# Order of the first rows and weights, idle products ahead of them, and the squares of the gating stage in one transformer kernel

## The chip, the cores and the metric

One core of a Trainium2 chip runs the whole kernel in one launch. The metric is the device time in microseconds (us) of that launch. TensorE (PE in the profile) multiplies, ScalarE (ACT) evaluates functions and copies, VectorE (DVE) does elementwise work, GpSimd (POOL) does a little elementwise work, and the queue of SyncE (SP) issues nearly all transfers from the chip's memory.

## The reference

Two blocks follow each other on one sequence of 512 positions and 2048 features, all in float32. Every row norm is an rms norm over the features.

```python
h = rmsnorm(x, norm_mix_g);  u = h @ w_in                 # 2048 -> 12288, ten parts
ya = b_g * causal_dwconv3(c_g * xa, conv_w) * silu(za)
log_f, kk = gates of fl;  o = hgrn2_chunked(silu(q), kk, iv, log_f)   # 8 heads
yb = head_norm(o) * hg_norm_g * silu(og)
m = sigmoid(ga) * (ya @ w_a_out) + sigmoid(gb) * (yb @ w_b_out)
x = x + m @ w_o
gate = sigmoid(rmsnorm(x, ple_norm_g) @ w_ple_gate)       # the gating stage
x = x + gate * (p @ w_ple_proj)
x = rmsnorm(x, final_norm_g)
# second block
h = rms_norm(x, g) * (1 + scale) + shift                  # scale, shift, gate from silu(c) @ w_ada
proj = h @ w_in_2                                         # attention (8 heads), retention (4 heads)
x = rms_norm(x + gate * (y @ w_out_2), final_gain_2)
```

## The kernel before, in words

Data lie transposed: a "row" k is 128 features on the partitions by 512 positions. Each float32 operand is split in two, a high part cast to the reduced type fp32r (XH for data, WH for weights) and the remainder (XL, WL). A product is three TensorE products: high with high, low data with high weights, high data with low weights.

The work is a list of groups (`_plan`, L153). A group multiplies 16 rows (8 or 2 for some) with 512 weight columns and fills four banks of the product memory, so a group of 16 rows is 16 x 4 x 3 = 192 products. A unit is two rows of weights, so a group has eight units and three unit buffers stand in WH and WL, four in RAW. `pe_dense` (L295) writes the products of a group in steps k = 0 to 15: in an even step k, rows k and k+1 into banks 0 and 1, in an odd step the same two rows into banks 2 and 3. With `fed=True` the rows are still being made while the group runs, so steps 0 and 1 take one row each into all four banks. For each row and bank the loop at L319 issues the three products one after the other. Ahead of the first it waits for both halves of the row (`xhi`, `xlo`), ahead of the third for WL.

`act_dense` (L338) casts WH on ScalarE (L354), `dve_dense` (L359) subtracts to get WL on VectorE (L375), and `sp_dense` loads RAW. Each goes through the same steps k. In a step it first makes the weight units that `hi_upto` (L201) or `lo_upto` (L205) asks for, then the rows of data that its feed asks for, and then one piece of each of two queues of side work (`Turns`, L113): `chores`, a piece every step, and `specials`, at the rate `pace`. Every engine executes its instructions in the written order, so what stands ahead in a step delays what stands behind it.

At the start (group ("fl", 0)) the rows are x itself times a gain: ScalarE casts XH (L454) and squares the row (L459), VectorE makes XL (L475) and adds up the squares (L483). `start_part` (L513) is the special that asks for rows faster than the group does, up to 16 rows by its seventh piece. It then runs the bounds of the gates (`bound_act`, `bound_dve`, nine tiny VectorE operations), and the first row norm: one product with ones (L399, `norm0_pe`), its `rsqrt_dve` (L410) and `rsqrt_act` (L403), and then the normed rows of the next group ("q", 0) (L500, L490, L504). TensorE issues nothing until the first rows and weights are there.

The gating stage is the groups ("gate", 0) to ("gate", 3), on eight units each. After each of them ScalarE evaluates four sigmoids (L1630), VectorE multiplies and adds into x (L1922, L1926), and ScalarE writes for each of the four new rows two squares (L1650), plain and times a gain. POOL adds each up (L2019) and the square buffers are single, so a square waits until POOL has added the one before. For the last group ScalarE makes four squares only (L1637), and TensorE takes them as they are. After group 2 VectorE makes nine small weight tiles WG (L1929 to L1935). Behind the last group TensorE sums the squares (L1453 to L1463, twelve records of 512 columns until the first sum is complete), `rsqrt_dve` and `rsqrt_act` with the key r_12 turn the sum into a factor, VectorE makes three tiny vectors GG, GF (L1939 to L1943), and then the rows of the second block follow (L1095, L1080, L1100) for ("qr", 0), which is a group with `fed=True`. `rsqrt_act` first waits for its input and then asks for its function table.

Of the kernel before, what the change touches and what calls it, by code (L numbers as in the profile page):

```python
# [199 lines left out]

def hi_upto(n, k):  # L201
    return min(n + AHEAD if n or k else 0, len(UNITS) - 1) + 1


def lo_upto(n, k):  # L205
    return min(hi_upto(n, k), n + AHEAD + k % 2 if n else 3)

# [9 lines left out]
def build(nc, xT, pT, vec, logits, cst, masks, ident, w_in, w_a, w_b, w_o, w_gate, w_proj,  # L217
# [77 lines left out]
    def pe_dense(name, xh, xl, ready, swap=False, kmap=None, fed=False, cols=slice(0, 512)):  # L295
# [6 lines left out]
        for k in range(nk):  # L302
            n = FIRST[name] + k // 2
            s = n % NSPL
            if fed and k < 2:
                work = [(k, i) for i in range(4)]
            else:
                work = [(k - k % 2 + j, i + k % 2 * 2) for i in range(2) for j in range(2)]
            for q, i in work:
# [9 lines left out]
                for j, (l, r) in enumerate(pairs):  # L319
                    if j == 0:  # L320
                        T.wait_ge(hi, (yield hi, n if n or q else "first"))
                        T.wait_ge(xhi, (yield xhi, (ready, kk)))
                        T.wait_ge(xlo, (yield xlo, (ready, kk)))
                        if q == 0 and gone[i]:
                            T.wait_ge(gone[i][0], (yield gone[i]))
                    if j == 2:
                        T.wait_ge(lo, (yield lo, n if n or q else "first"))
                    first, final = q == 0 and j == 0, q == nk - 1 and j == 2
                    ins = nc.tensor.matmul(bank[b][:, cols], l, r[:, cols], start=first, stop=final)  # L329
                    done = [(name, i)] * (j == 2 and q == nk - 1)  # L330
                    done += [("unit", n)] * (j == 2 and k % 2 == 1 and (q, i) == work[-1])
                    if done:
                        ins.then_inc(dense.sem, dense.step(*done))
# [68 lines left out]

    def rsqrt_act(key, m, y):  # L403
        A.wait_ge(dve, (yield dve, (key, "m")))
        A.use(LNEXP)
        nc.scalar.activation(y, m, ACT.Ln).then_inc(act.sem, act.step((key, "ln")))
# [20 lines left out]
    SC = sb("SC", [5, 512], F32, 73728 + 11 * 2048)  # L427
    xv = xT.rearrange("(k p) s -> p k s", p=128)
    XLOADS = ([0], [1], [2, 3], [4, 5, 6], [7, 8, 9, 10], [11, 12, 13, 14, 15])
    xload = {k: ld[f"x{ks[0]}"] for ks in XLOADS for k in ks}  # L430

# [18 lines left out]
    def feed_raw_act():  # L450
        A.wait_ge(ld["vec"], (yield ld["vec"], 0))
        for k in range(16):
            A.wait_ge(xload[k], (yield xload[k], 0))
            nc.scalar.activation(XH1[:, k], X0[:, k], ACT.Copy, scale=vcol("mix_g", k)  # L454
                                 ).then_inc(xhi.sem, xhi.step(("raw", k)))
            for j in range(k - 1 if k else 16, 16 if k == 15 else k):
                if j > 2:
                    A.wait_ge(dve, (yield dve, ("acc0", j - 2)))
                nc.scalar.activation(SC[:, j % 2 if j else 2], X0[:, j], ACT.Square  # L459
                                     ).then_inc(act.sem, act.step(("sq0", j)))  # L460
# [10 lines left out]
    def feed_raw_dve():  # L471
        V.wait_ge(ld["vec"], (yield ld["vec"], 0))
        for k in range(16):
# [4 lines left out]
            for j in range(k - 2, 16 if k == 15 else k - 1):  # L478
                if j > 0:
                    V.wait_ge(act, (yield act, ("sq0", j)))  # L480
                    if j > 1:
                        V.wait_ge(dve, (yield dve, ("acc0", j - 1)))
                    nc.vector.tensor_tensor(SC[:, 2], SC[:, 2], SC[:, j % 2], ALU.add  # L483
                                            ).then_inc(dve.sem, dve.step(("acc0", j)))
# [28 lines left out]
    def start_part(eng, bound, norm):  # L513
        for n in range(7):
            if eng in raw_feed:
                yield from raw_feed[eng].upto(min(16, 2 * n + 4))
            yield
        if bound:
            yield from bound
        yield  # L520
        yield
        if eng == "pe":
            yield
        yield from norm
        yield
        for n in range(1, 7):
            if eng in h_feed:
                yield from h_feed[eng].upto(n)
            yield
# [872 lines left out]
    def pe():  # L1402
        shared[0] = True
        turns = pe_turns
        turns.specials.append(start_part("pe", None, norm0_pe()))
        yield from pe_dense(("fl", 0), XH1, XL1, "raw", fed=True)
# [101 lines left out]
    def act_program():  # L1508
# [112 lines left out]
        for g in range(4):  # L1621
            yield from act_dense(("gate", g), g_feed["act"])
            for i in range(4):
# [3 lines left out]
                else:  # L1627
                    A.wait_ge(xlo, (yield xlo, ("g", 12 + i)))
                A.use(SIG)
                nc.scalar.activation(GT[:, i], bank[banks["gate", g][i]][:, :], ACT.Sigmoid  # L1630
                                     ).then_inc(ev_a.sem, ev_a.step((("gate", g), i)))
            for i in range(4):
                j = 4 * g + i
                A.wait_ge(dve, (yield dve, ("x2", j)))
                if g == 3:
                    A.wait_ge(dense, (yield dense, (("proj", 3), 3)))
                    nc.scalar.activation(SQ2[:, 2 + i], X1[:, j], ACT.Square  # L1637
                                         ).then_inc(act.sem, act.step(("sq2", j)))
                    continue
                for u in range(2):  # L1640
                    scale = vcol("fin_g", j) if u else 1.0
                    if j == 0:
                        A.wait_ge(side, (yield side, ("r_ple", "sum")))
                        dst = AC[:, u]
                    else:
                        A.wait_ge(dense, (yield dense, (("proj", 3), 3)))
                        if j > 1:
                            A.wait_ge(pool, (yield pool, ("acc2u", u, j - 1)))
                        dst = SQ2[:, u]
                    nc.scalar.activation(dst, X1[:, j], ACT.Square, scale=scale  # L1650
                                         ).then_inc(act.sem, act.step(("sq2u", u, j)))
        yield from rsqrt_act("r_12", NN[:, 0], R12)
# [87 lines left out]
        for h in range(2):  # L1740
# [10 lines left out]
            else:  # L1751
                yield from to_end(out_norm_act(1))

    def out_norm_act(h):
        if h == 0:
# [55 lines left out]
    def first_norm_dve():  # L1811
        yield from idle(4)
        V.wait_ge(dve, (yield dve, ("r_12", "r")))
        yield from rsqrt_dve("r_1", 1.0 / D, NN[:, 0], R1, NN[:, 2])

    def dve_program():
# [94 lines left out]
        for g in range(4):  # L1911
            yield from dve_dense(("proj", g))
            if g == 0:
                yield from rsqrt_dve("r_ple", 1.0 / D, NN[:, 0], NN[:, 1], NN[:, 2])
                turns.specials.append(rows_of(g_feed["dve"], 16))
        for g in range(4):
            yield from dve_dense(("gate", g), g_feed["dve"])
            for i in range(4):
# [8 lines left out]
                                        ).then_inc(dve.sem, dve.step(("x2", j)))  # L1927
            if g == 2:
                nc.vector.tensor_scalar(WG[:, 4], ONES[:, :], EPS, None, ALU.mult  # L1929
                                        ).then_inc(dve.sem, dve.step())  # L1930
                for i in range(4):
                    nc.vector.tensor_scalar(WG[:, i], ONES[:, :], vcol("fin_g", 12 + i), vcol("fin_g", 12 + i),
                                            ALU.mult, ALU.mult).then_inc(dve.sem, dve.step(("wg", i)))
                    V.wait_ge(dve, (yield dve, ("wg", i)))
                    nc.vector.tensor_scalar(WG[:, i], WG[:, i], EPS, None, ALU.add  # L1935
                                            ).then_inc(dve.sem, dve.step(*(["wg"] if i == 3 else [])))
        yield from rsqrt_dve("r_12", 1.0 / D, NN[:, 0], R12, NN[:, 2], eps=EPS * EPS)
        V.wait_ge(dve, (yield dve, "mod"))
        nc.vector.tensor_scalar(GG, MOD[:, 16:32], 1.0, None, ALU.add).then_inc(dve.sem, dve.step("gg0"))  # L1939
        V.wait_ge(dve, (yield dve, "gg0"))  # L1940
        nc.vector.tensor_tensor(GG, GG, vall("ng"), ALU.mult).then_inc(dve.sem, dve.step("gg"))
        V.wait_ge(dve, (yield dve, "gg"))
        nc.vector.tensor_tensor(GF, GG, vall("fin_g"), ALU.mult).then_inc(dve.sem, dve.step("gf"))  # L1943
        turns.specials.append(first_norm_dve())
# [220 lines left out]
```

## Time and profile before

| | us |
|---|---|
| median of 3 runs (lowest, highest) | 2627.98 (2627.77, 2628.41) |
| the profiled execution | 2625.84 |
| its span, from first to last instruction | 2624.5 |
| PE busy in the span | 2593.7 (99%) |
| DVE busy | 1265.5 (48%) |
| ACT busy | 892.0 (34%) |
| POOL busy | 73.7 (3%) |
| transfers | 309.18 MB, 118 GB/s on average |

Times of the rows below come from the one profiled execution. They start at the span's beginning. "PEld" is the load of the stationary operand on TensorE, which runs beside the products. A duration of TensorE is that of one pipelined product; products issued back to back start at a closer distance than their duration.

### The profile page before, as it was taken

How to read it: one execution, taken by the hardware profiler on the slowest of the kernel's cores; microseconds unless marked ns; L12 is line 12 of the kernel's file. 1: busy time of each engine (PE TensorE's matmuls, PEld its weight loads, DVE VectorE, ACT ScalarE, POOL GpSimd, SP SyncE). 2: the span in 40 equal slices, each digit the busy share in tenths (PEclk: the TensorE clock that was granted, in tenths of full speed). 3: DMA queues.
4: the chain of work that ended last, by engine and by line, in shares of the span. 5: the costliest groups of instructions: out<-in, count | busy, mean ns of one | idle time of the engine just before them, and what ended most of it. 6: DMA issues, size and time to landing. Idle time of an engine off the chain costs nothing.

```text
span 2624.5 us, 29678 instructions
## 1 busy us (share of the span) xinstructions
PE 2593.7 (99%) x12166; PEld 2095.4 (80%) x12166; DVE 1265.5 (48%) x2013; ACT 892.0 (34%) x1236; POOL 73.7 (3%) x64
## 2 busy tenths in 40 slices
PE   8999999999999999999999999999999999999998
PEld 7888888878888888888888888688777777777888
DVE  7556634468334555655443453552243434443425
ACT  5643324333222222222322443332232343433323
POOL 0000000000000000000001111100000000000000
PEclk9999999999999999999999999999999999999999
DMA  5322233222334666666442222234222222222424
GB/s 194 101 76 78 81 97 97 89 73 81 89 96 147 217 216 207 216 213 213 136 161 97 94 99 97 73 125 145 85 72 64 89 72 81 73 73 84 165 97 153
DMA packets 159976, 309.18 MB, mean 118 GB/s; under 512 B 11040, under 2 KB 15392, under 8 KB 158816
## 3 DMA queue, kind: packets, MB, share of 16 engines
q1 hardware_dynamic: 159040, 305.70, 36.1%
q8 instruction: 96, 1.57, 0.2%
q0 software_dynamic: 224, 1.15, 0.1%
q10 hardware_dynamic: 576, 0.43, 0.1%
q14 instruction: 40, 0.33, 0.0%
HBM read 298.84 MB, written 8.39 MB: 117 GB/s over the span
## 4 chain that ended last, share of the span: by engine, by line
PE 94%; DVE 2%; issue 2%; ACT 1%; DMA 0%; POOL 0%; SPq 0%; DVEq 0%; ACTq 0%; POOLq 0%
PE bank L329 87%; PE bank L1276 1%; PE bank L1167 1%; PE bank L1250 1%; PE bank L702 1%; PE bank L754 1%; PE bank L1265 1%; PE bank L1156 1%; PE bank L399 0%; DVE WL L375 0%; ACT WH L354 0%; DVE SC L483 0%; DMA X<-in_xT 0%; DVE Y L1980 0%; PE bank L692 0%
## 5 line engine op out<-in xcount | busy, mean ns | idle before, releaser
L329 PE MATMUL bank<-XH,WH 128*128 128x512 f32 (+1 forms) x2880 | 1145.6, 398 | 12.2 <-DVE XL L475 5.5
L329 PE MATMUL bank<-XH,WL 128*128 128x512 f32 (+1 forms) x2880 | 1111.7, 386 | 5.5 <-DVE WL L375 5.5
L329 PE MATMUL bank<-XL,WH 128*128 128x512 f32 (+1 forms) x2880 | 1109.9, 385 | 0.0
L375 DVE TENSOR_TENSOR WL<-RAW,WH 128x1024 fp32r<-128x1024 f32 x443 | 544.0, 1230 | 958.1 <-ACT WH L354 957.2
L354 ACT CAST WH<-RAW 128x1024 fp32r<-128x1024 f32 x443 | 463.9, 1049 | 1162.2 <-PE bank L329 1162.0
L329 PEld LDWEIGHTS bank<-XH,WH 128*128 128x128 f32 x2880 | 542.4, 188 | 135.1 <-issue 20.7
L329 PEld LDWEIGHTS bank<-XL,WH 128*128 128x128 f32 x2880 | 542.7, 188 | 119.3 <-issue 15.0
L329 PEld LDWEIGHTS bank<-XH,WL 128*128 128x128 f32 x2880 | 542.1, 188 | 116.9 <-DVE WL L375 7.2
L329 PE MATMUL bank<-WH,XH 128*128 128x512 f32 x384 | 155.6, 405 | 0.0
L329 PE MATMUL bank<-WL,XH 128*128 128x512 f32 x384 | 149.8, 390 | 0.0
L329 PE MATMUL bank<-WH,XL 128*128 128x512 f32 x384 | 149.5, 389 | 0.0
L1016 DVE CUSTOM_DVE_ANT_0 AST<-AST,CB 128x512 f32<-128x512 f32 x192 | 125.3, 687 | 10.8 <-DMA AST<-in_w_ada 10.8
L329 PE MATMUL bank<-YH,WH 128*128 128x512 f32 x256 | 101.0, 394 | 0.0
L329 PE MATMUL bank<-YH,WL 128*128 128x512 f32 x256 | 100.4, 392 | 0.0
L329 PE MATMUL bank<-YL,WH 128*128 128x512 f32 x256 | 99.5, 389 | 0.0
L329 PEld LDWEIGHTS bank<-WH,XL 128*128 128x128 f32 x384 | 72.2, 188 | 17.5 <-issue 3.1
L329 PEld LDWEIGHTS bank<-WH,XH 128*128 128x128 f32 x384 | 72.1, 188 | 17.4 <-issue 3.1
L329 PEld LDWEIGHTS bank<-WL,XH 128*128 128x128 f32 x384 | 72.1, 188 | 15.3
L1354 DVE CUSTOM_DVE_ANT_0 PP<-PP,CM 128x512 f32<-128x512 f32 x32 | 22.2, 692 | 79.9 <-ACT PP L1288 79.9
L1305 ACT COPY PT<-bank 128x512 f32<-128x512 f32 x32 | 18.7, 585 | 116.1 <-PE bank L1265 116.1
L329 PEld LDWEIGHTS bank<-YH,WL 128*128 128x128 f32 x256 | 48.1, 188 | 11.3
L329 PEld LDWEIGHTS bank<-YL,WH 128*128 128x128 f32 x256 | 48.1, 188 | 10.7
(252 smaller groups left out, 1634.5 us busy)
## 6 DMA issues: line engine op xcount, KB each, us to landing
RAW<-in_w_in SPq DMA_DIRECT2D x303, 512.0 KB, 3.6
AST<-in_w_ada SPq DMA_DIRECT2D x192, 256.0 KB, 4.1
RAW<-in_w_out SPq DMA_DIRECT2D x40, 512.0 KB, 3.5
RAW<-in_w_o SPq DMA_DIRECT2D x32, 512.0 KB, 3.5
RAW<-in_w_gate SPq DMA_DIRECT2D x32, 512.0 KB, 3.5
RAW<-in_w_a SPq DMA_DIRECT2D x16, 512.0 KB, 4.2
RAW<-in_w_b SPq DMA_DIRECT2D x16, 512.0 KB, 4.2
XT<-in_xT SPq DMA_DIRECT2D x4, 1024.0 KB, 7.4
```

What stands on the lines that cost most here:

```text
L329: ins = nc.tensor.matmul(bank[b][:, cols], l, r[:, cols], start=first, stop=final)
L354: nc.scalar.copy(WH[:, m % NSPL], RAW[:, m % NRAW]).then_inc(hi.sem, hi.step(m))
L375: nc.vector.tensor_tensor(WL[:, m % NSPL], RAW[:, m % NRAW], WH[:, m % NSPL].bitcast(F32), ALU.subtract).then_inc(lo.sem, lo.step(m))
L702: ins = nc.tensor.matmul(b[y:y + 64, 32 * n:32 * n + 32].rearrange("p (n x) -> p n x", x=h), t, late(t, lev), start=True, stop=True, tile_ ...
L754: ins = nc.tensor.matmul(b[:, 128 * c:512], VN[:, c, 128 * i:128 * i + 128], AT[:, 640 * c:512 * c + 512], start=c == 0, stop=c == 3)
L1016: nc.vector.tensor_tensor_reduce(AST[:, n % 3], AST[:, n % 3], CB[:, q % 2], 1.0, 0.0, ALU.mult, ALU.add, PART[:, n:n + 1]).then_inc(dve.s ...
L1156: nc.tensor.matmul(b[:, :], YY[:, 9 + 2 * r, 128 * c:128 * c + 128], YY[:, 8 + 2 * r], start=True, stop=True).then_inc(side.sem, side.step ...
L1167: ins = nc.tensor.matmul(b[:, :], V2[:, c, 256 * r + 128 * u:256 * r + 128 * u + 128], PT[:, c], start=c == 0, stop=c == 3)
L1250: nc.tensor.matmul(b[:, :], YY[:, h, 128 * i:128 * i + 128], K[:, j], start=True, stop=True).then_inc(side.sem, side.step(("as", h, i)))
L1265: ins = nc.tensor.transpose(b[:, 128 * c:128 * c + 128], PP[:, i % 2, 128 * c:128 * c + 128], IDN[:, :])
L1276: ins = nc.tensor.matmul(b[:, :], Vt[:, c, 128 * j:128 * j + 128], PT[:, c], start=c == 0, stop=c == 3)
L1354: nc.vector.tensor_tensor_reduce(P, P, CM[:, 2, 384 - 128 * i:896 - 128 * i], 1.0, 0.0, ALU.mult, ALU.add, st[:, 2:3]).then_inc(dve.sem, d ...
```

## The change

Six edits. Products of a fed group's first row are issued part by part over the four banks. The waits for XH and XL are separated. Rows and weight units of the first group are ordered anew on ScalarE and VectorE, the norm of the start comes ahead of the bounds, and a row's square is written later than the row, into four buffers. Eleven products of ones with ones, 128 columns each, stand ahead of the first group on TensorE, whose result is not read. In the gating stage the squares of groups 0 to 2 become a chore with one row in every second step of the next group, the weight tiles become a chore of group 1, and GG and GF move ahead of the stage. `rsqrt_act` asks for its table before it waits.

```diff
 def hi_upto(n, k):
+    if n < 2:
+        return k + 1
     return min(n + AHEAD if n or k else 0, len(UNITS) - 1) + 1
 def lo_upto(n, k):
-    return min(hi_upto(n, k), n + AHEAD + k % 2 if n else 3)
+    return hi_upto(n, k) if n < 2 else min(hi_upto(n, k), n + AHEAD + k % 2)
...
-            if fed and k < 2:
-                work = [(k, i) for i in range(4)]
+            if fed and k == 0:
+                work = [(0, i, (j,)) for j in range(3) for i in range(4)]
+            elif fed and k == 1:
+                work = [(1, i, (0, 1, 2)) for i in range(4)]
...
                     if j == 0:
                         T.wait_ge(hi, (yield hi, n if n or q else "first"))
                         T.wait_ge(xhi, (yield xhi, (ready, kk)))
-                        T.wait_ge(xlo, (yield xlo, (ready, kk)))
...
+                    if j == 1:
+                        T.wait_ge(xlo, (yield xlo, (ready, kk)))
...
     def rsqrt_act(key, m, y):
+        A.use(LNEXP)
         A.wait_ge(dve, (yield dve, (key, "m")))
-        A.use(LNEXP)
...
     # feed_raw_act, a row k of x
-            for j in range(k - 1 if k else 16, 16 if k == 15 else k):
-                if j > 2:
-                    A.wait_ge(dve, (yield dve, ("acc0", j - 2)))
-                nc.scalar.activation(SC[:, j % 2 if j else 2], X0[:, j], ACT.Square
+            for j in range(max(k - 2, 0) if k < 11 else k - 1, 16 if k == 15 else k if k > 9 else k - 1):
+                if j > 4:
+                    A.wait_ge(dve, (yield dve, ("acc0", j - 4)))
+                nc.scalar.activation(SC[:, SQ_AT[j % 4] if j else 2], X0[:, j], ACT.Square
...
     def start_part(eng, bound, norm):
-        for n in range(7):
+        for n in range(10):
             if eng in raw_feed:
-                yield from raw_feed[eng].upto(min(16, 2 * n + 4))
-            yield
-        if bound:
-            yield from bound
-        yield
-        yield
+                yield from raw_feed[eng].upto(2 * n + 2 if n < 4 else 4 + (4 * n + 1) // 3)
+            yield
         if eng == "pe":
             yield
         yield from norm
         yield
+        if bound:
+            yield from bound
         for n in range(1, 7):
...
     def pe():
+        T.wait_ge(dve, (yield dve, "ones"))
+        for n in range(11):
+            nc.tensor.matmul(bank[7][:, 0:128], ONES[:, :], ONES[:, :], start=True, stop=True)
...
-        yield from act_dense(("fl", 0), raw_feed["act"])
+        yield from act_dense(("fl", 0), raw_feed["act"], 1)
-        yield from dve_dense(("fl", 0), raw_feed["dve"])
+        yield from dve_dense(("fl", 0), raw_feed["dve"], 1)
...
     # act_program, after each of the groups ("gate", g)
-            for i in range(4):
-                ... (both squares of the row, each behind its waits)
+            if g < 3:
+                turns.chores.append(squares_act(g))
+                continue
+            yield from turns.finish(turns.chores)
+            ... (the four squares of g == 3)
+    def squares_act(g):
+        for j in range(4 * g, 4 * g + 4):
+            ... (the same two squares and waits)
+            yield
+            yield
...
     # dve_program
+    def last_weights_dve():
+        yield from idle(4)
+        ... (WG[4], then WG[i] in two operations, a yield after each i)
+        ... (wait for "mod", then GG, GG, GF, ahead of the loop over the gate groups)
         for g in range(4):
             yield from dve_dense(("gate", g), g_feed["dve"])
...
-            if g == 2:
-                ... (WG[4] and WG[i])
+            if g == 0:
+                turns.chores.append(last_weights_dve())
+        yield from turns.finish(turns.chores)
         yield from rsqrt_dve("r_12", 1.0 / D, NN[:, 0], R12, NN[:, 2], eps=EPS * EPS)
-        ... (wait for "mod", GG, GG, GF)
```

## Rows read from the trace of the kernel before

**Rows 1.** The page, part 1: busy time, share of span, instructions.
```profile
PE 2593.7 (99%) x12166; PEld 2095.4 (80%) x12166; DVE 1265.5 (48%) x2013; ACT 892.0 (34%) x1236; POOL 73.7 (3%) x64
```
**Rows 2.** Waits of PE, whole span: us in total, times, longest us.
```profile
PE bank L329 <- DVE XL L475: 5.5, 1, 5.5
PE bank L329 <- DVE WL L375: 5.5, 4, 2.3
PE bank L329 <- ACT WH L354: 0.5, 2, 0.3
```
**Rows 3.** Windows: stretch, busy us (x) by engine, granted clock, DMA share, GB/s.
```profile
35.10:37.90 2.80, 0.49 (x4) 0.06 (x2) 2.60 (x4) 0.63 (x1) 0.00 (x0) 1.00 0.01 3
1699.00:1702.50 3.50, 3.50 (x9) 2.76 (x10) 3.50 (x6) 1.45 (x2) 0.00 (x0) 0.51 0.00 0
```
**Rows 4.** Timeline of the start: start us, us, engine line op [idle before <-releaser].
```profile
0.84 0.17 DVE L1818 MEMSET ONES<- 128x128 f32 x1 [0.84 <-PEq L2158]
...
4.42 0.60 ACT L347 CAST WH<-RAW 128x512 fp32r<-128x512 f32 x1
...
5.53 0.77 PE L329 MATMUL bank<-XH,WH 128*128 128x512 f32 x1 [5.53 <-DVE XL L475]
...
9.50 0.40 PE L329 MATMUL bank<-XH,WH 128*128 128x512 f32 x1
```
**Rows 5.** Timeline, from the end of the first raw rows to the first norm.
```profile
36.59 1.22 DVE L375 TENSOR_TENSOR WL<-RAW,WH 128x1024 fp32r<-128x1024 f32 x1
37.73 0.16 DVE L550 TENSOR_TENSOR SM<-V 128x8 f32<-128x8 f32 x1
...
37.87 0.51 PE L329 MATMUL bank<-XH,WL 128*128 128x512 f32 x1 [2.31 <-DVE WL L375]
...
40.29 1.02 PE L399 MATMUL bank<-SC,ONES 128*128 128x512 f32 x2
...
41.63 0.68 DVE L412 TENSOR_SCALAR SC<-bank 128x512 f32<-128x512 f32 x1
...
45.86 1.29 DVE L500 TENSOR_TENSOR X<-X,R 128x512 f32<-128x512 f32 x2
```
**Rows 6.** Groups of DVE by line, 4 to 38 us: busy us, mean ns, idle before.
```profile
L475 DVE SCALAR_TENSOR_TENSOR XL<-X,V,XH 128x512 fp32r<-128x512 f32 x16 | 12.0, 749 | 8.6 <-ACT XH L454 8.6
L483 DVE TENSOR_TENSOR SC<-SC 128x512 f32<-128x512 f32 x15 | 10.3, 688 | 0.2
```
**Rows 7.** Timeline of PE: first products of ("q", 0) and of ("iv", 0).
```profile
54.89 0.40 PE L329 MATMUL bank<-XH,WH 128*128 128x512 f32 x1
...
98.46 0.39 PE L329 MATMUL bank<-WH,XH 128*128 128x512 f32 x1
```
**Rows 8.** Timeline of the gating stage, groups 2 and 3.
```profile
1606.60 0.50 PE L329 MATMUL bank<-XH,WL 128*128 128x512 f32 x1 [1.15 <-DVE WL L375]
...
1640.31 10.65 POOL L2019 TENSOR_TENSOR AC<-AC,SQ 128x512 f32<-128x512 f32 x8 [34.85 <-ACT SQ L1650]
...
1649.13 2.92 ACT L354 CAST WH<-RAW 128x1024 fp32r<-128x1024 f32 x3
...
1652.75 0.50 PE L329 MATMUL bank<-XH,WL 128*128 128x512 f32 x1 [1.80 <-DVE WL L375]
```
**Rows 9.** Timeline from the end of the gating stage into ("qr", 0).
```profile
1690.43 0.69 DVE L412 TENSOR_SCALAR NN<-bank 128x512 f32<-128x512 f32 x1 [2.91 <-PE bank L1457]
...
1691.15 1.28 ACT L64 ACT_TABLE_LOAD   x1 [2.96 <-DVE NN L412]
...
1695.83 0.17 DVE L1939 TENSOR_SCALAR SM<-MOD 128x16 f32<-128x16 f32 x1
...
1696.45 1.41 DVE L1095 SCALAR_TENSOR_TENSOR GT<-X,SM,NN 128x512 f32<-128x512 f32 x2
1697.24 1.38 ACT L1080 ACTIVATE XH<-GT,MOD 128x512 fp32r<-128x512 f32 x2 [2.57 <-DVE GT L1095]
...
1699.00 0.70 PE L329 MATMUL bank<-XH,WH 128*128 128x512 f32 x1 [4.31 <-DVE XL L1100]
```

More of the change, by code:

```diff
@@ L304, in pe_dense @@
             s = n % NSPL
-            if fed and k < 2:
-                work = [(k, i) for i in range(4)]
-            else:
-                work = [(k - k % 2 + j, i + k % 2 * 2) for i in range(2) for j in range(2)]
-            for q, i in work:
+            if fed and k == 0:
+                work = [(0, i, (j,)) for j in range(3) for i in range(4)]
+            elif fed and k == 1:
+                work = [(1, i, (0, 1, 2)) for i in range(4)]
+            else:
+                work = [(k - k % 2 + j, i + k % 2 * 2, (0, 1, 2)) for i in range(2) for j in range(2)]
+            for q, i, parts in work:
                 kk = kmap[q] if kmap else q
@@ L318, in pe_dense @@
                              (WL[:, s, q % 2, c], xh[:, kk])]
-                for j, (l, r) in enumerate(pairs):
+                for j in parts:
+                    l, r = pairs[j]
                     if j == 0:
@@ L330, in pe_dense @@
                     done = [(name, i)] * (j == 2 and q == nk - 1)
-                    done += [("unit", n)] * (j == 2 and k % 2 == 1 and (q, i) == work[-1])
+                    done += [("unit", n)] * (j == 2 and k % 2 == 1 and (q, i) == work[-1][:2])
                     if done:
@@ L428, in build @@
     xv = xT.rearrange("(k p) s -> p k s", p=128)
+    SQ_AT = (0, 1, 3, 4)
     XLOADS = ([0], [1], [2, 3], [4, 5, 6], [7, 8, 9, 10], [11, 12, 13, 14, 15])
@@ L482, in feed_raw_dve @@
                         V.wait_ge(dve, (yield dve, ("acc0", j - 1)))
-                    nc.vector.tensor_tensor(SC[:, 2], SC[:, 2], SC[:, j % 2], ALU.add
+                    nc.vector.tensor_tensor(SC[:, 2], SC[:, 2], SC[:, SQ_AT[j % 4]], ALU.add
                                             ).then_inc(dve.sem, dve.step(("acc0", j)))
@@ L1631, in act_program @@
                                      ).then_inc(ev_a.sem, ev_a.step((("gate", g), i)))
-            for i in range(4):
[L1633 to L1651, printed above, removed]
+            if g < 3:
+                turns.chores.append(squares_act(g))
+                continue
+            yield from turns.finish(turns.chores)
+            A.wait_ge(dense, (yield dense, (("proj", 3), 3)))
+            for i in range(4):
+                A.wait_ge(dve, (yield dve, ("x2", 12 + i)))
+                nc.scalar.activation(SQ2[:, 2 + i], X1[:, 12 + i], ACT.Square
+                                     ).then_inc(act.sem, act.step(("sq2", 12 + i)))
         yield from rsqrt_act("r_12", NN[:, 0], R12)
@@ L1752, in act_program @@
                 yield from to_end(out_norm_act(1))
+    def squares_act(g):
+        for j in range(4 * g, 4 * g + 4):
+            A.wait_ge(dve, (yield dve, ("x2", j)))
+            for u in range(2):
+                scale = vcol("fin_g", j) if u else 1.0
+                if j == 0:
+                    A.wait_ge(side, (yield side, ("r_ple", "sum")))
+                    dst = AC[:, u]
+                else:
+                    A.wait_ge(dense, (yield dense, (("proj", 3), 3)))
+                    if j > 1:
+                        A.wait_ge(pool, (yield pool, ("acc2u", u, j - 1)))
+                    dst = SQ2[:, u]
+                nc.scalar.activation(dst, X1[:, j], ACT.Square, scale=scale
+                                     ).then_inc(act.sem, act.step(("sq2u", u, j)))
+            yield
+            yield
     def out_norm_act(h):
@@ L1814, in first_norm_dve @@
         yield from rsqrt_dve("r_1", 1.0 / D, NN[:, 0], R1, NN[:, 2])
+    def last_weights_dve():
+        yield from idle(4)
+        nc.vector.tensor_scalar(WG[:, 4], ONES[:, :], EPS, None, ALU.mult
+                                ).then_inc(dve.sem, dve.step())
+        for i in range(4):
+            nc.vector.tensor_scalar(WG[:, i], ONES[:, :], vcol("fin_g", 12 + i), vcol("fin_g", 12 + i),
+                                    ALU.mult, ALU.mult).then_inc(dve.sem, dve.step(("wg", i)))
+            V.wait_ge(dve, (yield dve, ("wg", i)))
+            nc.vector.tensor_scalar(WG[:, i], WG[:, i], EPS, None, ALU.add
+                                    ).then_inc(dve.sem, dve.step(*(["wg"] if i == 3 else [])))
+            yield
     def dve_program():
@@ L1915, in dve_program @@
                 turns.specials.append(rows_of(g_feed["dve"], 16))
+        V.wait_ge(dve, (yield dve, "mod"))
+        nc.vector.tensor_scalar(GG, MOD[:, 16:32], 1.0, None, ALU.add).then_inc(dve.sem, dve.step("gg0"))
+        V.wait_ge(dve, (yield dve, "gg0"))
+        nc.vector.tensor_tensor(GG, GG, vall("ng"), ALU.mult).then_inc(dve.sem, dve.step("gg"))
+        V.wait_ge(dve, (yield dve, "gg"))
+        nc.vector.tensor_tensor(GF, GG, vall("fin_g"), ALU.mult).then_inc(dve.sem, dve.step("gf"))
         for g in range(4):
@@ L1927, in dve_program @@
                                         ).then_inc(dve.sem, dve.step(("x2", j)))
-            if g == 2:
-                nc.vector.tensor_scalar(WG[:, 4], ONES[:, :], EPS, None, ALU.mult
-                                        ).then_inc(dve.sem, dve.step())
-                for i in range(4):
[L1932 to L1936, printed above, removed]
-        yield from rsqrt_dve("r_12", 1.0 / D, NN[:, 0], R12, NN[:, 2], eps=EPS * EPS)
[L1938 to L1943, printed above, removed]
+            if g == 0:
+                turns.chores.append(last_weights_dve())
+        yield from turns.finish(turns.chores)
+        yield from rsqrt_dve("r_12", 1.0 / D, NN[:, 0], R12, NN[:, 2], eps=EPS * EPS)
         turns.specials.append(first_norm_dve())
```

## The prediction

> **What bounds the kernel now.** I read the page's busy shares first: TensorE is busy for 2593.7 of 2624.5 us [rows 1], so only its idle stretches and stretches at half clock can be won, some 31 us plus those. Then TensorE's waits over the whole span [rows 2], which name the stretches that the change touches: 5.5 us for XL at the start, four waits for WL with 5.5 us (the longest, 2.3, in the first group), two for WH with 0.5 us, and then the timeline at each place, and the granted clock beside it.
>
> The regular distance comes from ("q", 0), which runs without a break: (98.46 - 54.89)/192 = 0.227 us [rows 7]. An idle bracket counts from the modelled end of the last product (0.39 to 0.40 us after its start), so a wait costs its bracket plus 0.16 us, plus about 0.1 us for a slower first distance behind it, say 0.27 in all.
>
> **The start, products and clock.** The first product stands at 5.53 us, released by XL, though WH was cast at 4.42 + 0.60 = 5.02 [rows 4]. Nine products take until 9.50: 3.97 us in place of 9 x 0.227 = 2.04. That is the distance of 1.2 GHz, so 1.93 us are lost. The change removes the wait for XL from the first four products and puts eleven idle ones ahead, which can begin at about 1.1 us, when ONES is written [rows 4]. Their price: a pair of records of 512 columns takes 1.02 us with a duration of 0.59 each, so a start distance of 0.43 and 0.86 for one whole product at 2.4 GHz [rows 5]; 128 columns are a quarter of it, 0.21 us, or 0.43 at 1.2 GHz (estimates from that row). If the clock rises as long after the first activity as it did before, 3.97 us, it rises at 5.1, with 9.3 of the eleven done; the rest ends at about 5.5. The first real product starts there, at full clock. Gain 1.9 us. Bounds: the clock doesn't rise from such short products, and the eleven take 4.7 us and push the start to 5.8: 0.3 us lost; or it rises at once at the earliest the data allow, 2.3 us gained. I take 1.9, the value with the rise at the distance that the row has.
> The Trainium skill (TensorE: Matmul & The Clock Gate, Part 1) says that warming up is counted in time and not in matmuls, and that its moment varies from run to run; by that rule the rise comes after the eleven have ended in some runs, and each product until then takes twice its time. The trace has one start only and can't show that spread.
>
> **The start, order of rows.** In the first group TensorE stops once: 2.31 us until 37.87, for the WL of 36.59 [rows 5], 2.58 us in all by the rule above. That WL is unit 5, and it stood behind all sixteen rows, because `start_part` asks for 16 rows by its seventh piece. A row costs VectorE 0.75 us for XL and 0.69 for the sum [rows 6], about 1.26 when packed. With the new order unit 5 stands behind row 11 in place of row 15. Following the queues step by step with the same durations: unit 4's WH still waits for its transfer, which is queued behind all of x, and then WH is cast before rows 8 to 10. WL of units 4, 5 and 6 end near 25, 30 and 35 us, where TensorE wants them at 28, 33 and 39. So this stop goes: 2.6 us.
> What is late next is the norm. It stands on TensorE behind step 11, about 38.4 us; the last sum of squares ends near 37.9, so it doesn't wait. From its issue to the normed rows VectorE and ScalarE took 41.63 to 45.86, 4.2 us [rows 5], begun 0.6 us later than need be because a WL stood ahead. Now WL of unit 7 stands behind that chain. It ends near 38.4 + 1.1 + 4.2 + 1.15 = 44.9, and TensorE wants it about 6.5 us after the norm's issue, at 45.0. Behind it come the bounds (before: nine tiny operations from 37.73 [rows 5], about 2.2 us with ScalarE's answers), now in front of the normed rows and of units 8 to 10. These end at about 51.9, 55.6 and 61.7, wanted at 51.9, 55.7 and 61.3. Three margins of nearly nothing: I take 0.4 us lost. Bounds: nothing, or one stop as long as the old one, 2.6.
> ("q", 0) then starts near 50.8 in place of 54.89: the start is worth 1.9 + 2.6 - 0.4 = 4.1 us. After that ScalarE's casts are released unit by unit by TensorE, so all of the rest moves with it.
>
> **The gating stage.** ScalarE casts three WH in a row at 1649.13 because eight squares stood ahead of them, in lockstep with POOL's single buffer (eight additions, 10.65 us [rows 8]). TensorE then waits at unit 2 of the next group, once for WH and once for WL. Groups 2 and 3: brackets 1.15 and 1.80 for WL [rows 8], for WH two waits with 0.5 together [rows 2]. Group 1: what rows 2 leave for the fourth WL wait, 5.5 - 2.31 - 1.15 - 1.80 = 0.2. With 0.27 for each of the five waits: 3.65 + 1.35 = 5.0 us. As chores, a row's two squares come behind the casts, every second step of 2.7 us. POOL needs 10.65/4 = 2.7 us for a row's two additions and has 5.4. VectorE's weight tiles go to steps 4 to 7 of group 1, where it has nothing but one WL per two steps. ScalarE's next WH is cast right after the sigmoids, four steps before it is wanted. POOL's additions now lie beside WL subtractions; the one slowed WL costs nothing as it is wanted two steps later. Without that cover it would be one addition, 1.3 us, a unit. I take 5.0 gained; bounds 5.0 and 2.0 (one wait per boundary of 0.7 stays).
>
> **The border to the second block.** The sum is complete for VectorE at 1690.43. Then the function table, 1.28 us at 1691.15, stands in the chain [rows 9]; ScalarE is done with its squares 2 us earlier, so the load moves beside TensorE's products: 1.28. GG and GF stand between 1695.83 and 1696.45: 0.62. XH of the first row is then ready 1.90 us earlier, at 1697.24 + 0.71 - 1.90 = 1696.05, and the first product needs only that. It starts at about 1696.25 in place of 1699.00: 2.75 us. XL of row 0 follows 0.8 us behind XH, and four products take 0.9: at full clock just in time; row 3 is wanted at 1702.6 and ready at 1701.9. Bounds: 1.9 (if the start still hangs on XL) and 2.75; I take 2.75.
> The clock: in 1699.00 to 1702.50 the granted clock is 0.51 [rows 3], so 1.2 GHz, after TensorE had done nothing for 4.31 us [rows 9]. The other idle stretch, 2.31 us [rows 5], left it at 1.00 [rows 3]. The new one is about 1.6 us, on the side of the second. Eight intervals took 3.48 in place of 1.82 us: 1.6 gained; bounds 0 and 1.6.
> The same page of the Trainium skill (HAM oscillation) warns of idle gaps in TensorE's work as what brings the low clock back; the two stretches above agree with a limit that lies between them.
>
> Border: 2.75 + 1.6 = 4.35 us.
>
> **Sum.** 4.1 + 5.0 + 4.35 = 13.45 us. The profiled execution took 2625.84, its span 2624.5; both would be 13.4 less, 2612.4 and 2611.1. The runs' median is 2627.98, 2.1 above the profiled one, in which I see nothing that the change touches: 2627.98 - 13.45 = 2614.5.
> Other fed groups ("wb", "wo", "out") only get their first row's waits later, and their banks up to 1.4 us sooner, which the bank turnover has room for: nothing.
>
> **Rivals.**
> (a) *The clock doesn't follow.* One or both half-clock stretches stay: 1.6 at the border gives 2616.1, 1.9 to 2.2 at the start 2616.4 to 2616.7, both up to 2618.3. For: there is one row only of a rise and one of a fall, and idle products of 128 columns are not in the trace. Against: TensorE is as busy with them as with others. The moment that the rule above leaves open belongs here too.
> (b) *VectorE becomes the bound at the start.* The norm's chain and the bounds now stand ahead of units 7 to 10; if each comes late, TensorE stops again and gets back what it gained, 2.6 us or, with the bounds' 2.2 on the way, the whole 4.1: 2617.1 to 2618.6. For: margins under 0.5 us. Against: TensorE itself releases that chain, so it doesn't grow.
> (c) *The waits were hidden anyway*, or the chores move them to the last group, where ScalarE must finish them before the final squares: no change beyond the start's half, 2623 to 2628. Against: the chores are through by step 8 of sixteen.
> (d) *Slower.* The casts fall into lockstep with TensorE: with less lead in units 0 to 3 each unit is cast, subtracted and used in turn, and WH plus WL, 1.0 + 1.2 us, stand open for every unit. It takes over the sign from 13.45/2.2 = 6 units on; over the sixteen of ("fl", 0) and ("q", 0) it costs 35 us, so 2650. Against: from unit 4 on `hi_upto` is as it was, and ScalarE and VectorE sat idle 8.6 us for each other in the first 38 us [rows 6].
>
> **How the numbers follow.** Forecast 0.62, with its own range 2612.5 to 2616; (a) 0.18; (b) 0.13; (c) 0.04; (d) 0.03. The range holds the forecast, (a) and most of (b): 2611.5 to 2618. A change under 0.2% (5.3 us) can't be told from none. The forecast, (a) and (b) are all beyond it: faster 0.93, same 0.04, slower 0.03.
>
> **What would show it.** Right: first dense product near 5.5 with distances of 0.23 at once; no stop before the norm; ("q", 0) starting near 50.8; no waits for WH or WL in the gating stage; no table load between the first sum and its logarithm; TensorE idle for 1.5 to 2 us at the border, at a granted clock of 1.00. Wrong: distances of 0.43 after 5.5 or at the border (a); waits for WL between 44 and 62 us (b); waits at the gating stage's group starts (c).

## The result, and the profile after

The changed kernel takes 2612.01 us (median of 4 runs, 2611.78 to 2612.64), the kernel before 2628.19 beside it (4 runs, 2627.77 to 2630.15). The ratio is 0.9937, 95% interval 0.9920 to 0.9955: 16.2 us less. The profiled execution of the changed kernel is its slowest, 2612.64, with a span of 2611.3; that of the kernel before was faster than its runs. Between the two spans lie only 13.2 us. "Idle" below is the time in brackets in a row of a profile: from the modelled end of TensorE's last product to the next start.

Waits of TensorE, whole span (us in total, times, longest), for [rows 2]:
```profile
PE bank L1270 <- ACT PP L1302: 2.1, 2, 1.0
PE bank L335 <- issue: 1.6, 1, 1.6
PE bank L335 <- DVE Y L2001: 1.5, 2, 1.2
PE bank L1412 <- DVE ONES L1845: 1.1, 1, 1.1
```
Ahead of the attention one wait for a row is left, the 1.6 us at the border (listed as "issue"), and a short one behind it, at the ninth row of ("qr", 0). The timeline of the start, for [rows 4, 5, 7]:
```profile
1.06 5.06 PE L1412 MATMUL bank<-ONES 128*128 128x128 f32 x22 [1.06 <-DVE ONES L1845]
...
4.48 0.60 ACT L353 CAST WH<-RAW 128x512 fp32r<-128x512 f32 x1
...
5.77 1.74 PE L335 MATMUL bank<-XH,WH 128*128 128x512 f32 x4
...
7.35 1.09 PE L335 MATMUL bank<-XL,WH 128*128 128x512 f32 x4
...
39.41 1.02 PE L405 MATMUL bank<-SC,ONES 128*128 128x512 f32 x2
...
40.46 0.69 DVE L418 TENSOR_SCALAR SC<-bank 128x512 f32<-128x512 f32 x1 [1.66 <-PE bank L405]
...
47.82 1.29 DVE L507 TENSOR_TENSOR X<-X,R 128x512 f32<-128x512 f32 x2
...
51.26 1.10 PE L335 MATMUL bank<-XH,WH 128*128 128x512 f32 x4
...
51.53 1.22 DVE L381 TENSOR_TENSOR WL<-RAW,WH 128x1024 fp32r<-128x1024 f32 x1
...
53.12 0.62 PE L335 MATMUL bank<-XH,WL 128*128 128x512 f32 x2
```
The idle products run at 0.43 us each (two records of 0.21), and the first four dense ones take 1.58 us until the next four start, in place of 0.91: the granted clock rose at 7.02, 6.0 us after TensorE's first activity at 1.06. In the profile before it rose at 9.48, 4.0 us after the first product. ("q", 0) starts at 51.26, 3.63 earlier. WL of unit 8 ends at 52.75, 0.4 us before it is wanted.

The gating stage's group 3, for [rows 8]. The cast follows the last sigmoid, the squares come behind it:
```profile
1633.06 0.60 ACT L1638 ACTIVATE GT<-bank 128x512 f32<-128x512 f32 x1 [0.76 <-PE bank L335]
...
1633.55 1.05 ACT L360 CAST WH<-RAW 128x1024 fp32r<-128x1024 f32 x1
...
1634.49 0.63 ACT L1764 ACTIVATE SQ<-X 128x512 f32<-128x512 f32 x1
...
1635.20 2.37 POOL L2040 TENSOR_TENSOR AC<-AC,SQ 128x512 f32<-128x512 f32 x1 [24.60 <-ACT SQ L1764]
1635.21 1.22 DVE L381 TENSOR_TENSOR WL<-RAW,WH 128x1024 fp32r<-128x1024 f32 x1
```
The border, for [rows 9]. The table is loaded beside the products, and the first product follows XH:
```profile
1679.49 1.28 ACT L64 ACT_TABLE_LOAD   x1
...
1681.72 0.69 DVE L418 TENSOR_SCALAR NN<-bank 128x512 f32<-128x512 f32 x1 [2.92 <-PE bank L1465]
...
1682.45 0.63 ACT L412 ACTIVATE NN<-NN 128x512 f32<-128x512 f32 x1 [1.68 <-DVE NN L418]
...
1686.74 1.39 ACT L1085 ACTIVATE XH<-GT,MOD 128x512 fp32r<-128x512 f32 x2 [2.06 <-DVE GT L1100]
...
1687.56 1.17 PE L335 MATMUL bank<-XH,WH 128*128 128x512 f32 x4 [1.58 <-issue]
```
And the granted clock around it (stretch, busy by engine in the order PE, PEld, DVE, ACT, POOL, then clock, DMA share, GB/s), for [rows 3]:
```profile
1685.50:1687.60 2.10, 0.52 (x3) 0.07 (x1) 1.94 (x4) 0.86 (x2) 0.00 (x0) 1.00 0.00 0
1687.60:1692.00 4.40, 4.40 (x20) 3.61 (x21) 4.40 (x7) 1.97 (x3) 0.00 (x0) 1.00 0.00 0
```
Where the 13.3 us between the two profiles arise, by the start of the same dense product in both: 3.6 up to ("iv", 0), nothing more until the second gating group ("gate", 1), then 0.5, 2.0 and 2.65 at its three boundaries, 4.3 at the border (2.74 of idle time, 1.56 of half clock) and 0.25 at the ninth row behind it, and nothing from there to the end.

### The profile page after: what moved, and what is told of

Read it like the earlier page. It is cut to its first block, busy times and chain, and to the rows that moved or that the text cites. A ratio compares the mean times of both kernels' runs of the same rounds, so it can differ in the third digit from the quotient of the medians.

```text
span 2611.3 us, 29657 instructions
## 1 busy us (share of the span) xinstructions
PE 2594.0 (99%) x12188; PEld 2097.4 (80%) x12188; DVE 1259.8 (48%) x2013; ACT 889.7 (34%) x1236; POOL 79.0 (3%) x64
## 3 DMA queue, kind: packets, MB, share of 16 engines
q0 software_dynamic: 224, 1.15, 0.1%
## 4 chain that ended last, share of the span: by engine, by line
PE 99%; DVE 1%; ACT 0%; issue 0%
PE bank L335 91%; PE bank L1281 1%; PE bank L1172 1%; PE bank L1255 1%; PE bank L707 1%; PE bank L759 1%; PE bank L405 1%; PE bank L1270 1%; PE bank L1161 1%; PE bank L1412 0%; DVE Y L2001 0%; PE bank L697 0%; PE bank L715 0%; DVE X L1800 0%; PE bank L729 0%; PE bank L1512 0%
```

## The experiments

Twelve kernels. Median (lowest to highest) of n runs, and the median of the kernel before on the same chip:

| kernel | us | n | before | ratio, 95% |
|---|---|---|---|---|
| b_again | 2627.79 (2625.75 to 2630.21) | 11 | 2627.70 | 1.0001, 0.9992 to 1.0010 |
| b_idle | 2628.18 (2626.11 to 2630.12) | 11 | 2627.70 | 1.0000, 0.9992 to 1.0009 |
| b_order | 2626.34 (2624.05 to 2627.23) | 11 | 2627.70 | 0.9997, 0.9988 to 1.0006 |
| b_start | 2620.92 (2618.97 to 2624.17) | 11 | 2628.41 | 0.9973, 0.9964 to 0.9982 |
| b_gate | 2623.45 (2620.61 to 2624.49) | 11 | 2627.98 | 0.9980, 0.9971 to 0.9989 |
| b_border | 2625.25 (2624.55 to 2628.60) | 11 | 2627.98 | 0.9989, 0.9981 to 0.9998 |
| a_noidle | 2613.32 (2613.06 to 2613.44) | 5 | 2627.70 | 0.9945, 0.9932 to 0.9959 |
| a_oldorder | 2617.36 (2616.51 to 2617.63) | 5 | 2628.41 | 0.9957, 0.9945 to 0.9970 |
| a_fedold | 2615.09 (2614.66 to 2616.59) | 5 | 2627.98 | 0.9951, 0.9937 to 0.9964 |
| a_gateold | 2617.58 (2616.80 to 2619.22) | 5 | 2628.41 | 0.9960, 0.9947 to 0.9972 |
| a_tablelate | 2615.23 (2613.04 to 2615.40) | 5 | 2627.98 | 0.9947, 0.9935 to 0.9960 |
| a_best | 2611.70 (2611.42 to 2612.38) | 5 | 2628.41 | 0.9937, 0.9924 to 0.9949 |

The interval of a ratio is about 2.5 us wide to each side, with five runs 3.4. So b_idle and b_order can't be told from none by their times; there the profiles decide. What the kernels named a_ lose is said against the changed kernel's 2612.01, which ran on another chip; the median of the kernel before differs by up to 0.7 us between the chips.

**b_again**: before, unchanged.

> The kernel before, once more, for a second and third start of it. Theory S (the moment at which the clock rises varies from run to run, and the profiled execution of before had an early one, 3.97 us after the first product): this profile shows more than nine products at the distance of 0.43 us, up to sixteen, and the times scatter by 1 to 2 us between 2626 and 2628.5. Rival U (the 2.1 us between the profiled execution and the median of before come from something else, the same in each run): nine products at 0.43 again, and all times near 2628.

The clock rose at 10.31, 4.7 us after the first product at 5.59, against 4.0 in the profile before; at half clock the 0.8 us later cost 0.4. But the times scatter over 4.5 us. S is right in kind and its place is wrong: over all fourteen profiles the rise came 2.9 to 6.0 us after TensorE's first activity, which is worth about 1.5 us at half clock. U falls too.

**b_idle**: before with the idle products.
```diff
+        T.wait_ge(dve, (yield dve, "ones"))
+        for n in range(11):
+            nc.tensor.matmul(bank[7][:, 0:128], ONES[:, :], ONES[:, :], start=True, stop=True)
```

> The kernel before with the eleven idle products alone. By the two profiles the first dense product then stands at 5.8 us, 0.25 later, and three dense products are slow in place of nine: 1.0 us faster, 2627 beside 2628.2. Theory S: the median gains more than the profile shows, 1.5 to 2.5 us, because late rises of the clock are what the products take away. Rival U: 1.0 us. Rival V (the idle products give nothing, the row's order does it all): 0 or 0.3 us slower.

V comes nearest, for a reason that it didn't name. The products work: the clock rose at 4.16, the first dense product starts at 5.66 at full clock, and the tenth is 1.6 us ahead of the profile before. TensorE then runs into rows and units that aren't made yet, and is slowed at 39 us; at ("iv", 0) it is 2.0 us behind. Timeline of PE, then windows as above:
```profile
12.61 0.50 PE L329 MATMUL bank<-XH,WH 128*128 128x512 f32 x1 [0.87 <-ACT WH L354]
...
13.87 0.51 PE L329 MATMUL bank<-XH,WL 128*128 128x512 f32 x1 [0.52 <-DVE WL L375]
...
38.44 0.79 PE L329 MATMUL bank<-XH,WL 128*128 128x512 f32 x1 [2.30 <-DVE WL L375]
```
```profile
38.50:41.90 3.40, 3.40 (x9) 2.68 (x10) 2.14 (x9) 1.44 (x4) 0.00 (x0) 0.53 0.54 154
...
1656.00:1659.50 3.50, 3.50 (x10) 2.68 (x10) 1.02 (x1) 0.00 (x0) 0.00 (x0) 0.53 0.78 258
...
1702.60:1707.40 4.80, 4.77 (x11) 3.80 (x12) 4.80 (x7) 1.44 (x2) 0.00 (x0) 0.50 0.04 8
```
Behind the same 2.3 us of idle time the clock had stayed at 1.00 in the profile before [rows 3]; the second window stands behind the 1.8 us in gating group 3, where that profile was at full clock too. This is what formed theory F. The third window is the border: the half clock lasts until 1707.4 there, 4.8 us of work, where the profile before had 3.4. b_gate shows the same.

**b_order**: before with `hi_upto`, `lo_upto`, the row feeds, the four square buffers and `start_part` of the change.

> The kernel before with the new order of rows, squares and weight units in the first group alone (hi_upto, lo_upto, the row feeds, the four square buffers, the norm ahead of the bounds). Theory: the stop of 2.3 us at 35 us goes and nothing comes in its place, 2.6 us faster, (q, 0) starts at 52.3 in place of 54.9. Rival (b) of the prediction: a stop comes back at units 7 to 10, 44 to 62 us, and less than 1 us is left.

Half right: the stop at 35 us is gone, but one comes back as the rival says, at WL of unit 8:
```profile
54.59 0.50 PE L331 MATMUL bank<-XH,WL 128*128 128x512 f32 x1 [0.93 <-DVE WL L377]
```
It is the third product of ("q", 0). In the changed kernel the part order asks for WL with the ninth, 1.4 us later. The clock also rose 1.7 us later here than in the profile before (11.14 against 9.48), and fell at 1653 us, behind the 1.8 us of gating group 3.

**a_noidle**: after without the idle products.

> The changed kernel without the idle products. Theory by the profiles: the first dense product then stands at about 5.15 us, since it needs only XH and WH, and some 9 of the products are slow, so 0.6 to 1.2 us slower than the changed kernel, 2613. Theory S: 1.5 to 2.5 us slower in the median. Rival V: nothing, or 0.6 us faster as the start comes earlier.

1.3 us slower in the medians, 0.75 in the profiles, with 0.4 us of scatter: the first dense product stands at 5.25, and the clock rose at 9.30. As the profiles said, and the times don't need S. But the two profiles drew unlike rises, 4.0 us after the first activity here and 6.0 in the changed kernel, so 0.75 us isn't what the products are worth in every execution.

**b_gate**: before with the squares and weight tiles as chores.

> The kernel before with the gating stage's squares and weight tiles as chores, nothing else. Theory: the five waits go, 5.1 us in the profile (the part of the stage in the profile of the changed kernel). Theory F, from the second batch of profiles (a stop of TensorE of about 2 us is followed by 3.4 us at half clock in some executions and not in others; each costs 1.6 us): two stops fewer, so the median gains more than 5.1, some 6 us, 2621.7, and the times scatter less than the 4 us of the kernel before. Rival: the clock doesn't depend on these stops, then exactly 5.1 and the same scatter.

4.5 us in the medians, 5.4 between the fastest runs on that chip. The five waits are gone, and over the gating stage the same products gain 5.1 us on the profile before: the theory's size. Its extra in the median didn't come (the interval, 2.9 to 7.6 us, leaves it open), and the scatter stayed at 3.9 us: in the profiled execution the clock fell behind the stop at 36 us and at the border all the same. This profile also bears out b_idle without idle products: its clock rose early, at 8.83, and TensorE ran into two waits, of 0.40 and 0.53 us at 13 and 14 us, which the profile before doesn't have.

**b_border**: before with the table load first, and GG and GF ahead of the stage.
```diff
     def rsqrt_act(key, m, y):
+        A.use(LNEXP)
         A.wait_ge(dve, (yield dve, (key, "m")))
-        A.use(LNEXP)
```

> The kernel before with the table load ahead of the wait and with GG and GF ahead of the stage, nothing else. Theory: 1.28 + 0.62 = 1.9 us less idle time at the border, 2.8 us in place of 4.7. Whether the 3.4 us at half clock behind it go: by my prediction they go in each execution (3.5 us faster in all), by theory F only in some (between 1.9 and 3.5 in the median, scatter of 2 us or more).

2.7 us, within theory F's span, though the interval (0.5 to 5.0 us) holds the prediction's 3.5 too. The border's idle time is 1.8 us shorter, 2.5 in place of 4.3, and in the profiled execution the clock still fell behind it, and behind gating group 3 as well. So what the expectation drew from the prediction, that the half clock goes in each execution, doesn't hold.

**a_tablelate**: after with that diff taken back.

> The changed kernel with the table load behind the wait again. Theory: the border's idle time grows by 1.28 us to 3.2, so 2613.3 at least. Theory F: in part of the executions the clock falls behind it, which costs 1.6 more there: times in two heaps, 2613.3 and 2614.9. Rival (a limit between 2.3 and 4.3 us, the same in each execution): one heap, scatter of 0.5 us.

3.2 us slower, and in line with F's two heaps, from five runs: one at 2613.04 with a mean clock of 0.999, four from 2614.88 to 2615.40, three of them at 0.998. The profile of a run of the upper heap, with 2.9 us of idle time ahead of 1688.74:
```profile
1685.50:1689.50 4.00, 1.13 (x4) 0.67 (x4) 3.77 (x7) 1.75 (x3) 0.00 (x0) 1.00 0.00 0
1689.50:1692.90 3.40, 3.40 (x10) 2.62 (x9) 3.40 (x5) 1.44 (x2) 0.00 (x0) 0.51 0.00 0
```

**a_fedold**: after with the parts of the first row in the old order and both waits ahead of the first.
```diff
-                work = [(0, i, (j,)) for j in range(3) for i in range(4)]
+                work = [(0, i, (0, 1, 2)) for i in range(4)]
...
+                        T.wait_ge(xlo, (yield xlo, (ready, kk)))
```

> The changed kernel with the first row's products in the old order (high, XL and WL of a bank in turn, both halves of the row waited for ahead of the first). Theory: WL of unit 8 comes late at the first row of (q, 0), as it does in the kernel before with the new order alone (a stop of 1.09 us there), and the border loses the 0.75 us by which XH leads XL: 1.8 us slower, 2613.8. Rival: the part order is worth nothing beyond the border, 0.8 us.

3.1 us slower. The profile has the wait for WL of unit 8 again (0.92 us idle until 53.01, 1.1 lost), 2.52 us idle at the border in place of 1.58, and 0.25 more at the ninth row of ("qr", 0); 2.5 in all, with the span at 2613.8. No clock fell behind the 2.52 here, where b_border's did. Two of five runs lie 1.5 to 1.9 above the rest.

**b_start**: before with all edits of the start.

> The kernel before with all three edits of the start (idle products, new order of rows and units, products of the first row part by part), the gating stage and the tables as before. The part order also reaches the border, 0.75 us. Theory: the three need each other, since the idle products alone ran into two waits for rows (1.0 and 0.7 us) and the order alone into one at unit 8 (1.1 us): by the two profiles 3.6 us at the start, 0.8 at the border and, with one stop fewer, less half clock, so 4.4 to 6 us in the median, 2622 to 2623.5, where the parts alone gave 0 and 1.4. Rival: the parts don't need each other, then about 2 us, 2626.

7.5 us (interval 4.7 to 9.5), more than expected. The profile gives 6.8: 4.1 at the start, the rest at the border. This fastest run has no fall at all, even behind 3.37 us of idle time at the border; 1.6 of its 6.8 us is the half clock that the profile before had there.

**a_oldorder**: after with the order of rows, squares and units taken back.

> The changed kernel with the old order of rows, squares and units in the first group. Theory: the stop of 2.5 us behind 35 us comes back, and with the idle products the rows and units are late at 11 to 14 us by some 1.5 us more; half clock behind one of them in part of the executions (1.6 us): 4 to 5.5 us slower, 2616 to 2617.5, with a scatter of 2 us. Rival: only the stop, 2.6 us, 2614.6.

5.4 us slower, the theory's upper end: waits of 1.52 and 0.52 us at 12 and 14, a third of 0.7 at 38, and half clock from 14.23 to 17.65. The profiled run is the fastest, 3.9 slower in span. Timeline of PE:
```profile
12.45 0.50 PE L333 MATMUL bank<-XH,WH 128*128 128x512 f32 x1 [1.52 <-ACT WH L358]
...
13.71 0.50 PE L333 MATMUL bank<-XH,WL 128*128 128x512 f32 x1 [0.52 <-DVE WL L379]
...
14.74 0.63 PE L333 MATMUL bank<-XH,WL 128*128 128x512 f32 x1
```

**a_gateold**: after with squares and weight tiles in their old place.

> The changed kernel with the squares and weight tiles of the gating stage in their old place. Theory: five waits of 5.1 us in all come back; two of them are stops of 1.3 and 2.0 us, and behind the longer one the clock falls in part of the executions: 5.1 to 6.7 us slower, 2617.1 to 2618.7, in two heaps. Rival: 5.1 us in each execution, scatter of 0.5 us.

5.6 us slower, from 4.8 to 7.2. Over the gating stage its profile loses 5.2 us, the theory's size, with no fall of the clock. The five runs show no clear heaps, and the highest lies above the theory's span.

**a_best**: after with two changes.
```diff
-        for n in range(11):
+        for n in range(9):
...
     # first_norm_act and first_norm_dve
-        yield from idle(4)
+        yield from idle(13)
```

> The changed kernel with nine idle products in place of eleven, and with the second norm of the border (r_1, 4.1 us of VectorE between the rows of (qr, 0)) moved from the fifth to the fourteenth piece of that group. Theory: the first dense product stands 0.5 us earlier, at half clock, which is worth 0.3 us; the wait of 0.5 us at the ninth row of (qr, 0) goes, as all sixteen rows are made by then: 0.8 us faster, 2611.2. Rival: with fewer idle products the clock rises later and takes it back, and the norm only moves the wait to the next group: 2612.

2611.70, 0.3 below the changed kernel's median, on another chip, so not told apart by the times. In the profile the wait at the ninth row is gone, worth 0.4 us. The first dense product stands at 5.51, and the clock had risen at 5.46, where the changed kernel's profile has 7.02: 0.8 us at the start, most of which may be the luck of one execution. The span is 2610.0.

## Why the prediction was right, step by step

The profile was met to 0.2 us (span 2611.3 for 2611.1). The median, 2612.01 for 2614.5, was missed by 2.5 us and lies below the forecast's own range, inside the whole range.

**The border** was right to a tenth in the two profiles: from VectorE's first operation on the sum to the first product it took 1699.00 - 1690.43 = 8.57 us and takes 5.84, so 2.73 for 2.75. With the clock at 1.00, 4.3 for 4.35.

**The gating stage**: 5.1 for 5.0. Shown from both sides by b_gate and a_gateold. The cover named for POOL's additions wasn't needed: the addition takes 2.37 us beside a WL subtraction, which keeps its 1.22. One part of the mechanism was left out. Behind group 2 WL waits not only for WH: VectorE's nine operations on the weight tiles end after the first WH is cast (1649.13 and about 1 us), while behind group 1 WL follows WH at once. Timeline of DVE before:
```profile
1604.69 4.11 DVE L375 TENSOR_TENSOR WL<-RAW,WH 128x1024 fp32r<-128x1024 f32 x3 [7.87 <-ACT WH L354]
...
1651.33 0.23 DVE L1935 TENSOR_SCALAR WG<-WG 128x128 f32<-128x128 f32 x1
1651.48 3.49 DVE L375 TENSOR_TENSOR WL<-RAW,WH 128x1024 fp32r<-128x1024 f32 x3
```
That boundary was worth 2.65 us and the one without tiles 2.0, so the tiles' own share is some 0.65 us (an estimate from the two). Squares and tiles were moved together in each run, so no run separates them.

**The start**: the stop at 35 us was 2.6 and is gone. The lateness of 0.4 didn't come, WL of unit 8 is on time by 0.4 us. The term that was mis-sized is the clock's, 1.9: nine dense products on, the gain is 1.0. The prediction let the clock rise as long after the first activity as before, and here it took 2 us longer. In the six other profiles with eleven idle products it rose 2.9 to 5.8 us after them, so 1.9 was one value of several. That the sum for the profile, 13.45, met 13.2 is in part luck: 0.9 too much for the clock stands against 0.4 for a lateness that didn't come, 0.25 at the ninth row, which the sum had left out, and 0.1 in the gating stage.

**The step that failed** is about the median: "2.1 above the profiled one, in which I see nothing that the change touches". The change touches it. The forecast took it that a stop of 2.31 us leaves the clock at 1.00 and that a limit lies between that and 4.31. The fourteen profiles, by the idle time of a stop:

| idle, us | profiles with that stop | half clock at it or behind it |
|---|---|---|
| 1.6 (border) | 5 | 0 |
| 1.8 (gating group 3) | 7 | 3 |
| 2.3 (start) | 5 | 2 |
| 2.5 (border) | 2 | 1 |
| 2.9 (border) | 1 | 1 |
| 3.4 (border) | 1 | 0 |
| 4.3 (border) | 5 | 5 |

a_oldorder adds a fall behind waits of 1.5 and 0.5 us close to each other. So no limit holds in each execution for stops of 1.8 to 3.4 us: the same stop is followed by half clock in some executions and not in others. A fall lasted 3.4 us and cost 1.6 to 1.7 us; at the border of b_idle and b_gate it lasted 6.8 us, 4.8 and 5.1 of them with TensorE at work. The profiled execution before had one fall, at the border.

The runs of the kernel before spread from 2625.8 to 2631.3, and the mean clock of a run goes with it. Of the 74 in the experiments 27 have 0.998 and 2626.6 us on average, 36 have 0.997 and 2628.4, and 11 have 0.996 and 2630.5: steps of about one fall. The changed kernel has one stop of 1.6 us left where the kernel before had four of 1.15 to 4.31 (besides three of 1.0 to 1.2 in the attention that both have), and all its four runs lie at 0.999 within 0.9 us. The medians are 3.0 us further apart than the spans. 2.35 of them is that the profiled execution before was faster than its median, about what one or two falls more would cost: these no longer come. The other 0.6 is that the changed kernel's profiled run was its slowest; its cause stays open. How often each stop is followed by a fall wasn't measured, and a run without a profile shows its falls only through its mean clock.

**Rivals.** (b) was the near one: alone (b_order) the order does turn into a stop at unit 8, and the part order, which the prediction priced at the border and at the first product only, is what holds it off. Taken out (a_fedold), it costs 3.1 us in the medians, of which the profile has 1.1 at unit 8. That term was missing. (a) holds for the start in part: 0.9 us. (c) and (d) didn't come.

The edits of the start aren't additive. By the profiles, up to ("iv", 0), the idle products alone lose 2.0 us (1.6 of it a fall of the clock), the order alone gains 0.7 and the three together 4.1; the part order wasn't tried alone. In the medians idle products, order, stage and tables alone give +0.5, -1.4, -4.5 and -2.7, the first two not clear of noise, and the three of the start together -7.5.

## What to carry to other kernels

Feeding TensorE earlier was worth nothing here until what it eats was made in the order of need, and a late operand may be covered by no more than the order of a row's products. Take the effect of an edit in the best executions and in the median separately: a stop cost its length always and a stretch at half clock in some executions only. One profile shows one such execution; read the mean clock of the other runs beside it. Ask for function tables and tiny constants before the wait, not behind it.

## What the runs showed of the hardware

- Behind a stop of TensorE with 1.8 to 2.5 us of idle time the granted clock was 0.5 in some executions and 1.00 in others (the table above). The low stretch was 3.4 us long, at the border of b_idle and b_gate 6.8. It set in up to 1.6 us after the work had begun again (the stop in b_idle that ended at 1654.80; the first slow product is at 1656.36), and at the border of b_idle 2.0 us before it did (1700.6, work from 1702.63).
- From TensorE's first activity to the rise of the clock it took 2.9 us (a_oldorder) to 6.0 (after), with idle products of 128 columns as without them (3.1 in b_gate, 5.6 in b_order).
- The Trainium skill (TensorE: Matmul & The Clock Gate, Part 1) calls the moment of the rise variable from run to run, and the traces agree, with the 2.9 to 6.0 us above. The fall varied too: these runs show it, and the prediction took it as fixed.
- POOL's addition of two 128x512 tiles took 2.37 us beside VectorE's subtraction for WL, against 1.27 at the shortest before; VectorE's `tensor_scalar` on 128x128 took 1.2 to 1.3 us beside POOL's additions in place of 0.2 to 0.3 (1642 to 1651 us before).
